# Gate and up of both feed-forward blocks by a seven-product scheme, the fourth product of a group ahead of the next group's sixth

## The chip, the cores and the metric

The kernel runs on one core of a Trainium2 chip. The metric is the device time of one execution in microseconds (us), the median of several runs; lower is better. The core has TensorE (matrix products, with weight loads of its own), VectorE (DVE in the rows), ScalarE (ACT), GpSimd (POOL) and SyncE (SP), whose queue starts most DMA transfers. Each engine works through its instructions in order; engines wait for each other on semaphores.

## What is computed

The reference is one step of a hybrid decoder layer on 512 prompt tokens and 8 sample tokens (520 columns here), width 1024. The change touches the two feed-forward blocks only:

```python
def swiglu_half(x, g_pre, w_gate, w_up, w_down, g_post):
    h = rmsnorm(x, g_pre)
    y = (jax.nn.silu(h @ w_gate) * (h @ w_up)) @ w_down
    return x + 0.5 * rmsnorm(y, g_post)
...
xp = swiglu_half(xp, *ffn1)
xp, sp = token_mixing(xp, ...)
xp = swiglu_half(xp, *ffn2)
```

The hidden width is 2816, that is 22 groups of 128 columns of w_gate and w_up. Everything is 32-bit.

## The kernel before

Activations lie transposed: x is [128 partitions, 8 chunks of 128 channels, 520 tokens]. TensorE multiplies in a 32-bit format of less precision, so every operand is held as a high part (a rounded copy, made by ScalarE) and a low part (the difference, made by VectorE), and every product is three: high x high, high weight x low, low weight x high. The norm factor of a token is applied after the products, to gate and to the hidden value.

`ffn(which, ...)` (from line 447) is one feed-forward block, called for which = 0 and 1 with the mixer between. Its weights come as blocks of [128, 8 x 128] (512 KB), gate and up in turn; the down projection has 16 blocks of [128, 11 x 128] (704 KB). A block goes through these steps, all by the block's number: `load_block` (L108) on SyncE's queue, into one of two raw buffers `w_raw`, as soon as the low part of the block two before is made; `split_high` (L129) on ScalarE; `split_low` (L133) on VectorE; `block_products` (L150, L152, L154) on TensorE: for each of 8 chunks, 2 token halves x 3 products of 260 columns into two PSUM banks, 48 matmuls a block, 96 for gate and up of one group.

Per group VectorE takes gate times factor out of PSUM (L592), ScalarE makes silu (L514), GpSimd multiplies by the factor again (L493), VectorE multiplies with up (L602), ScalarE makes the high part `a_high` (L518), VectorE the low part (L607). The first two groups are written out, the 20 others are a rolled loop (`pe.Fori(2, KF)` and its counterparts on the other engines). With the first block `start_products` (L288 to L292) takes the first group as its inputs come in. The `down` loop follows, then a second norm and the residual; x stays in SBUF throughout a block.

## Time and profile before

| | us |
|---|---|
| median of 3 runs | 1528.04 (1527.54 to 1530.77) |
| the profiled execution, first to last instruction (span) | 1525.5 |
| TensorE busy | 1485.0 (97%), 12552 matmuls |
| weight loads of TensorE busy (beside the matmuls) | 1367.5 (90%) |
| VectorE busy | 670.1 (44%) |
| ScalarE busy | 494.4 (32%) |
| GpSimd busy | 209.9 (14%) |
| rolled gate and up groups, first and second block | 230.7 each |

No time of the profiled execution besides its span is recorded; the median of the runs is 2.5 us above it. "Busy" counts the time in which an engine has at least one instruction under way; matmuls overlap each other, so their mean duration is more than what one of them adds. The share of an engine is a mean over stages with different limits. The granted clock of TensorE is 0.990 of 2.4 GHz on the mean.

### The profile page before, as it was taken

What the parts mean: (1) busy time and instruction counts of PE and PEld (TensorE: products, weight loads), DVE (VectorE), ACT (ScalarE), POOL (GpSimd) and SP (SyncE); (2) the same over time, 40 slices, a digit from 0 to 9 for tenths busy, and PEclk for the clock granted to TensorE, in tenths of its full rate; (3) what the DMA queues carried; (4) which work ended last, traced back from release to release, by engine and by line L of the source; (5) the groups of instructions that cost most, each with busy time, mean ns of one, the idle gap of its engine ahead of it and who ended that gap; (6) DMA issues with size and microseconds to landing.
All of it is one profiled execution on the core that took longest, in us unless ns stands there. A gap on an engine that the chain in (4) does not pass through costs nothing. (4 is left out here: it accounts for less than half of the span.)

```text
span 1525.5 us, 31235 instructions
## 1 busy us (share of the span) xinstructions
PE 1485.0 (97%) x12552; PEld 1367.5 (90%) x12552; DVE 670.1 (44%) x1021; ACT 494.4 (32%) x724; POOL 209.9 (14%) x199
## 2 busy tenths in 40 slices
PE   8999999999999999999998999989999999999996
PEld 7999999999888888877876887769989999999996
DVE  5333333222645765244476533456364434433224
ACT  6222223222521345221134333342353322323222
POOL 0111111000162000323200220021001111110000
PEclk9999999999999999999999999989999999999998
DMA  4222223222569978999997667837213222232221
GB/s 160 94 96 82 96 88 106 96 95 82 198 230 359 327 272 288 368 329 334 380 344 252 198 210 253 283 129 261 84 47 105 84 96 86 93 99 97 95 95 56
DMA packets 113366, 268.80 MB, mean 176 GB/s; under 512 B 15562, under 2 KB 18251, under 8 KB 112515
## 3 DMA queue, kind: packets, MB, share of 16 engines
q1 hardware_dynamic: 106610, 243.27, 46.5%
q0 software_dynamic: 6240, 23.28, 4.3%
q8 instruction: 64, 1.05, 0.3%
q10 hardware_dynamic: 432, 1.05, 0.2%
q14 instruction: 20, 0.16, 0.0%
HBM read 253.29 MB, written 14.26 MB: 175 GB/s over the span
## 5 line engine op out<-in xcount | busy, mean ns | idle before, releaser
L129 ACT ACTIVATE w_high<-w_raw 128x1024 fp32r<-128x1024 f32 (+1 forms) x179 | 199.6, 1116 | 705.6 <-PE psum L154 680.4
L133 DVE TENSOR_TENSOR w_low<-w_raw,w_high 128x1024 fp32r<-128x1024 f32 (+1 forms) x179 | 231.8, 1296 | 431.6 <-ACT w_high L129 430.2
L150 PE MATMUL psum<-h_high,w_high 128*128 128x260 f32 x1344 | 270.6, 282 | 0.6 <-DVE w_low L133 0.6
L154 PE MATMUL psum<-h_high,w_low 128*128 128x260 f32 x1344 | 270.9, 283 | 0.0
L152 PE MATMUL psum<-h_low,w_high 128*128 128x260 f32 x1344 | 270.4, 283 | 0.0
L150 PEld LDWEIGHTS psum<-h_high,w_high 128*128 128x128 f32 x1344 | 207.2, 188 | 1.5 <-DVE w_low L133 1.5
L154 PEld LDWEIGHTS psum<-h_high,w_low 128*128 128x128 f32 x1344 | 207.2, 188 | 0.0
L152 PEld LDWEIGHTS psum<-h_low,w_high 128*128 128x128 f32 x1344 | 206.6, 188 | 0.0
L493 POOL TENSOR_TENSOR silu<-silu,factor 128x520 f32<-128x520 f32 x44 | 79.1, 1798 | 505.3 <-ACT silu L514 505.3
L150 PE MATMUL psum<-mix_h_high,w_high 128*128 128x260 f32 x672 | 140.5, 290 | 1.2 <-issue 1.2
L152 PE MATMUL psum<-mix_h_low,w_high 128*128 128x260 f32 x672 | 136.4, 284 | 0.9 <-issue 0.9
L154 PE MATMUL psum<-mix_h_high,w_low 128*128 128x260 f32 x672 | 136.5, 285 | 0.4 <-issue 0.4
L150 PE MATMUL psum<-a_high,w_high 128*128 128x260 f32 x660 | 133.1, 283 | 0.0
L154 PE MATMUL psum<-a_high,w_low 128*128 128x260 f32 x660 | 132.7, 282 | 0.0
L152 PE MATMUL psum<-a_low,w_high 128*128 128x260 f32 x660 | 132.5, 282 | 0.0
L150 PEld LDWEIGHTS psum<-mix_h_high,w_high 128*128 128x128 f32 x672 | 104.3, 190 | 18.0 <-issue 17.6
L154 PEld LDWEIGHTS psum<-mix_h_high,w_low 128*128 128x128 f32 x672 | 104.8, 190 | 1.2 <-issue 1.2
L152 PEld LDWEIGHTS psum<-mix_h_low,w_high 128*128 128x128 f32 x672 | 104.7, 190 | 0.4 <-issue 0.4
L152 PEld LDWEIGHTS psum<-a_low,w_high 128*128 128x128 f32 x660 | 101.8, 188 | 0.0
L154 PEld LDWEIGHTS psum<-a_high,w_low 128*128 128x128 f32 x660 | 101.6, 188 | 0.0
L150 PEld LDWEIGHTS psum<-a_high,w_high 128*128 128x128 f32 x660 | 101.5, 188 | 0.0
L1058 POOL DMA_INDIRECT scores<-in_cache_logf,logf_rows x64 | 66.8, 1043 | 24.1 <-issue 17.7
(366 smaller groups left out, 2003.4 us busy)
## 6 DMA issues: line engine op xcount, KB each, us to landing
kv_ring<-in_cache_k SPq DMA_DIRECT2D x256, 256.0 KB
kv_ring<-in_cache_v SPq DMA_DIRECT2D x256, 256.0 KB
w_raw<-in_w_gu SPq DMA_DIRECT2D x86, 512.0 KB
w_raw<-in_w_dn SPq DMA_DIRECT2D x32, 704.0 KB
w_raw<-in_w_proj SPq DMA_DIRECT2D x44, 512.0 KB
spill<-h_f POOLq DMA_DIRECT2D x20, 260.0 KB
gates<-spill POOLq DMA_DIRECT2D x16, 260.0 KB, 4.2
w_raw<-in_w_merge SPq DMA_DIRECT2D x8, 512.0 KB
```

The costliest lines, as they stand in the source:

```text
L129: act.activation(w_high[:, u, 0:nk, :], w_raw[:, u, 0:nk, :], ACT.Copy).then_inc(high_done, 1)
L133: dve.tensor_tensor(w_low[:, u, 0:nk, :], w_raw[:, u, 0:nk, :], w_high[:, u, 0:nk, :].bitcast(F32), ALU.subtract).then_inc(low_done, 1)
L150: pe.matmul(out[h], w_high[:, u, k, :], high[:, k0 + j, tok[h]], start=s, stop=False)
L152: pe.matmul(out[h], w_high[:, u, k, :], low[:, k0 + j, tok[h]], start=False, stop=False)
L154: mm = pe.matmul(out[h], w_low[:, u, k, :], high[:, k0 + j, tok[h]], start=False, stop=e)
L493: pool.tensor_tensor(sg[:, u, :], sg[:, u, :], factor[:, :], ALU.mult).then_inc(gate_late, 1)
L1058: pool.indirect_dma_start(sc[:, t * P + 1:(t + 1) * P + 1], None, a["cache_logf"], bass.IndirectOffsetOnAxis(ap=idx[:, r, t:t + 1], axis=0 ...
```

## The change

Of each group n from 2 to 21, the product of the weights (gate and up, each cut into even and odd chunks) with the activations (even and odd chunks, each cut into two token halves) is a product of 2 x 2 blocks. The eight block products become seven, in the manner of Strassen and Winograd, with sums of weights and of activations made beforehand and sums of results behind:

- P1 and P2 (together "PA", 24 matmuls), P3, P4, P5, P6, P7 (12 matmuls each): 84 a group. P1 and P2 use the even and odd chunks of gate with the first half of the tokens.
- Sums of weights: S1, S2 (VectorE), S3, S4 (GpSimd), each 4 x 128 columns. Each unit's high part is made by ScalarE (`unit_high`) and its low part by VectorE (`unit_low`), in a ring of 4 slots of 4 chunks, PA in 8 chunks of its own.
- Sums of activations t(0) to t(3), once per block, by GpSimd out of `xw` (x times the norm weights, made by ScalarE), each 4 x 260 columns, then high and low parts.
- Sums of results: g1 = P1 + P2, u2 = P1 + P6, c22, c12 on VectorE and ScalarE; silu and factor in halves of 260 columns ("g1f", "silu1", "late1", "g2f", "silu2", "c22f"); the hidden value in halves ("hid1", "hid2").
- Order on TensorE for each n: PA(n), P7(n-1), P5(n), P4(n-1), P6(n), P3(n-1).
- All steps are counted on one semaphore per engine (`gu_act`, `gu_dve`, `gu_pool`, `gu_used`); A, V, G and at give the count behind a step. The rolled loops become straight-line code. The raw weights, their parts and the half results lie over `w_raw`, `w_high`, `w_low`, x, `h_f`, `root` and `sq`; x is therefore loaded again behind the stage, and in the second block written to DRAM before it.
- The start of the down projection is rewritten to fit (`down_start`), and the mixer's merge counts on other semaphores, with the same steps.

The core of the diff:

```diff
+def unit_order():
+    order = [("gate", 1), ("up", 1)]
+    for n in range(G0, KF + 1):
+        for kind, m in (("PA", n), ("P7", n - 1), ("P5", n), ("P4", n - 1), ("P6", n), ("P3", n - 1)):
+            if G0 <= m < KF:
+                order.append((kind, m))
+    return order
...
+def ring_slots(order):
+    slot, free, r, held = {}, {}, 0, []
+    for i, (kind, n) in enumerate(order):
+        if kind in ("gate", "up"):
+            at = (0, 0)
+        elif kind == "PA":
+            at = (0, 8)
+        else:
+            c = 8 + 4 * ((r - 5 * NG7) % 4)
...
+BANK_A = {n: (n + 2) % 3 for n in range(G0, KF)}
+BANK_B = {n: 5 + n % 2 for n in range(G0, KF)}
+BANK_C = {n: 3 + n % 2 for n in range(G0, KF)}
...
-            nb = n0 + 2 * KF
+            nb = n0 + 2
...
+                c_raw = over(f"second_raw{which}", [P, 2, KD, P], F32, ah, 2 * T)
+                c_high = over(f"second_high{which}", [P, 2, KD, P], F32R, ah, 6 * T)
+                c_low = over(f"second_low{which}", [P, 2, KD, P], F32R, al, 2 * T)
+                sg = over(f"silu{which}", [P, 2, T], F32, ah, 10 * T)
+                xw = over(f"x_weighted{which}", [P, KD, T], F32, ah, 12 * T)
+                hf = over(f"hidden{which}", [P, 2, T], F32, al, 6 * T)
+                t2 = over(f"sum_two{which}", [P, KD // 2, HT], F32, al, 8 * T)
...
+                raws = [over(f"raw_even{which}", [P, 2, KD, P], F32, "w_raw"),
+                        over(f"raw_odd{which}", [P, 2, KD, P], F32, "x", 4 * T)]
...
+                def operand(kind, j):
+                    if kind == "P1":
+                        return h_high[:, 2 * j, first_half], h_low[:, 2 * j, first_half]
+                    if kind == "P2":
+                        return h_high[:, 2 * j + 1, first_half], h_low[:, 2 * j + 1, first_half]
+                    if kind == "P3":
+                        return h_high[:, 2 * j + 1, second_half], h_low[:, 2 * j + 1, second_half]
+                    if kind == "P7":
+                        return h_high[:, 2 * j, second_half], h_low[:, 2 * j, second_half]
+                    if kind == "P5":
+                        return t_hi[:, j, :], t_lo[:, j, :]
+                    if kind == "P6":
+                        return t_hi[:, 4 + j, :], t_lo[:, 4 + j, :]
+                    return t_hi[:, 8 + j, :], t_lo[:, 8 + j, :] if j < 2 else t4_rest[:, j - 2, :]
...
-                    load_stream(sp, w_gu, 2 * KF, n0, KD, first=False)
-                    load_stream(sp, w_dn, 2 * KD, nb, NKD)
...
+                    sp.wait_ge(low_done, n0 + 2)
+                    load(G0, 0)
+                    load(G0, 1)
+                    if which == 1:
+                        for k in range(KD):
+                            sp.wait_ge(x_new, r0 - KD + k + 1)
+                            sp.dma_start(a["x_spill"][:, k, :], x[:, k, :]).then_inc(x_back, 16)
+                        sp.wait_ge(x_back, 32 + 16 * KD)
+                    sp.wait_ge(h_low_done, m0 + KD)
+                    sp.wait_ge(norm_sq, (norm_n + 1) * KD)
+                    sp.wait_ge(gu_act, A("xw", KD - 1))
+                    load(G0 + 1, 0)
+                    load(G0 + 1, 1)
+                    for n in range(G0 + 2, KF):
+                        sp.wait_ge(gu_pool, G("S4", n - 2))
+                        load(n, 0)
+                        sp.wait_ge(gu_dve, V("P4", n - 2))
+                        load(n, 1)
+                    sp.wait_ge(gu_pool, G("S4", LAST - 1))
+                    sp.wait_ge(gu_dve, V("P4", LAST - 1))
+                    load_block(sp, w_dn, 0, nb, 0, NKD)
+                    sp.wait_ge(gu_used, at("PA", LAST))
+                    load_block(sp, w_dn, 1, nb + 1, 1, NKD)
+                    sp.wait_ge(gu_dve, V("low", LAST))
+                    sp.dma_start(x[:, :, :], a["x"] if which == 0 else a["x_spill"]).then_inc(x_back, 16)
+                    load_stream(sp, w_dn, 2 * KD, nb, NKD, first=False)
...
+                    def sum_three(n):
+                        pool.wait_ge(gu_in[2 * (n % 2)], arrived(n))
+                        pool.wait_ge(gu_in[2 * (n % 2) + 1], arrived(n))
+                        if n > G0:
+                            pool.wait_ge(gu_dve, V("P7", n - 1))
+                        pool.tensor_tensor(s34[:, 0, :, :], even(gate(n)), even(up(n)), ALU.subtract).then_inc(gu_pool, 1)
...
+                    def sum_four(n):
+                        pool.wait_ge(gu_dve, V("S2", n))
+                        if n > G0:
+                            pool.wait_ge(gu_dve, V("P3", n - 1))
+                        pool.tensor_tensor(s34[:, 1, :, :], s12[:, 1, :, :], odd(gate(n)), ALU.subtract).then_inc(gu_pool, 1)
...
+                    pool.wait_ge(gu_act, A("xw", KD - 1))
+                    pool.tensor_tensor(xe1, xe1, xe2, ALU.subtract).then_inc(gu_pool, 1)
+                    pool.wait_ge(gu_pool, G("t", 0))
+                    pool.tensor_tensor(t2[:, :, :], xo2, xe1, ALU.add).then_inc(gu_pool, 1)
+                    late(0)
+                    pool.wait_ge(norm_rec, norm_n + 1)
+                    sum_three(G0)
+                    pool.tensor_tensor(xe2, xo2, xe2, ALU.subtract).then_inc(gu_pool, 1)
+                    late(1)
+                    pool.wait_ge(gu_pool, G("t", 1))
+                    pool.tensor_tensor(xo1, xo1, t2[:, :, :], ALU.subtract).then_inc(gu_pool, 1)
+                    sum_four(G0)
+                    for n in range(G0, KF):
+                        if n >= G0 + 2:
+                            gate_second(n - 2)
+                        if n > G0:
+                            sum_three(n)
+                            sum_four(n)
+                        gate_first(n)
+                        if n > G0:
+                            up_second(n - 1)
+                        gate_first_late(n)
...
+                    def unit_high(kind, n):
+                        slot, free = SLOT[kind, n], FREE[kind, n]
+                        if free:
+                            act.wait_ge(gu_used, u0 + free)
...
+                    def second_sum(n):
+                        act.wait_ge(gu_used, at("P6", n))
+                        if n >= G0 + 2:
+                            act.wait_ge(gu_dve, V("c12", n - 2))
+                        act.activation(u2[n % 2], psum[:, BANK_A[n], 0:HT], ACT.Copy).then_inc(gu_act, 1)
...
+                    silu(0)
+                    high(0)
+                    act.wait_ge(block_used, n0 + 2)
+                    unit_high("PA", G0)
+                    sum_high(0, t_hi[:, 0:4, :], xe1)
+                    unit_high("P5", G0)
+                    sum_high(1, t_hi[:, 4:8, :], t2[:, :, :])
+                    silu(1)
+                    unit_high("P6", G0)
+                    high(1)
+                    act.wait_ge(gu_used, at("up", 1))
+                    sum_high(2, T3_HIGH, xe2)
+                    sum_high(3, t_hi[:, 8:12, :], xo1)
+                    if which == 1:
+                        act.wait_ge(x_back, 32 + 16 * KD)
+                    for n in range(G0, KF):
+                        second_product(n)
+                        if n >= G0 + 2:
+                            gate_second_silu(n - 2)
+                        if n > G0:
+                            unit_high("P3", n - 1)
+                        if n < LAST:
+                            unit_high("PA", n + 1)
+                        unit_high("P7", n)
+                        gate_first_silu(n)
+                        fifth_product(n)
+                        second_sum(n)
+                        if n < LAST:
+                            unit_high("P5", n + 1)
+                        if n >= G0 + 2:
+                            hidden_high(n - 2)
+                        if n < LAST:
+                            unit_high("P6", n + 1)
+                        unit_high("P4", n)
...
+                    def sum_one(n):
+                        dve.wait_ge(gu_in[2 * (n % 2) + 1], arrived(n))
+                        if n > G0:
+                            dve.wait_ge(gu_dve, V("P5", n - 1))
+                            dve.wait_ge(gu_dve, V("S2", n - 1))
+                        dve.tensor_tensor(s12[:, 0, :, :], even(up(n)), odd(up(n)), ALU.add).then_inc(gu_dve, 1)
...
+                    def up_second(n):
+                        dve.wait_ge(gu_used, at("P7", n))
+                        dve.wait_ge(gu_act, A("p5", n))
+                        dve.tensor_tensor(c22[n % 2], psum[:, BANK_A[n], 0:HT], c22[n % 2], ALU.subtract).then_inc(gu_dve, 1)
...
+                    for n in range(G0, KF):
+                        gate_first(n)
+                        if n >= G0 + 2:
+                            hidden_second(n - 2)
+                        if n < LAST:
+                            sum_one(n + 1)
+                        if n > G0:
+                            up_second(n - 1)
+                            unit_low("P3", n - 1)
+                        if n < LAST:
+                            unit_low("PA", n + 1)
+                        unit_low("P7", n)
+                        if n < LAST:
+                            unit_low("P5", n + 1)
+                        if n >= G0 + 2:
+                            hidden_low(n - 2)
+                        if n < LAST:
+                            sum_two(n + 1)
+                        if n > G0:
+                            hidden_first(n - 1)
+                        if n < LAST:
+                            unit_low("P6", n + 1)
+                        if n > G0:
+                            gate_second(n - 1)
+                        unit_low("P4", n)
...
+                    def products(kind, bank, slot, j, start):
+                        hi, lo = operand(kind, j)
+                        out = psum[:, bank, 0:HT]
+                        pe.matmul(out, wh[:, slot, :], hi, start=start, stop=False, skip_group_check=True)
+                        pe.matmul(out, wh[:, slot, :], lo, start=False, stop=False, skip_group_check=True)
+                        return pe.matmul(out, wl[:, slot, :], hi, start=False, stop=j == 3, skip_group_check=True)
...
+                    def unit(kind, n):
+                        slot = SLOT[kind, n]
+                        pe.wait_ge(gu_dve, V(kind, n))
...
+                            for j in range(4):
+                                products("P1", BANK_A[n], slot + 2 * j, j, j == 0)
+                                mm = products("P2", BANK_B[n], slot + 2 * j + 1, j, j == 0)
...
+                            elif kind == "P6":
+                                pe.wait_ge(gu_dve, V("g1", n))
...
+                            elif kind == "P7":
+                                pe.wait_ge(gu_act, A("u2", n))
...
+                                if kind == "P4":
+                                    pe.wait_ge(gu_dve, V("c22", n))
```

## Rows read from the trace of the kernel before

**Rows 1.** Windows: busy us of each engine in the first rewritten stretch, then PEclk, DMA share, GB/s
```profile
33.90:264.60 230.70, 230.70 (x1923) 230.70 (x1922) 89.49 (x100) 66.01 (x80) 36.69 (x20) 1.00 0.28 94
```

**Rows 2.** Timeline (start us, us, what, [idle <-releaser]): TensorE in the loop; VectorE and TensorE at 1141
```profile
102.95 0.40 PE L154 MATMUL psum<-h_high,w_low 128*128 128x260 f32 x2
103.19 0.40 PE L150 MATMUL psum<-h_high,w_high 128*128 128x260 f32 x2
...
1141.02 1.23 DVE L133 TENSOR_TENSOR w_low<-w_raw,w_high 128x1024 fp32r<-128x1024 f32 x1 [0.49 <-ACT w_high L129]
1142.30 0.51 PE L150 MATMUL psum<-h_high,w_high 128*128 128x260 f32 x2 [0.58 <-DVE w_low L133]
```

**Rows 3.** Groups by form (xcount | busy us, mean ns | idle): VectorE, then ScalarE
```profile
L133 DVE TENSOR_TENSOR w_low<-w_raw,w_high 128x1024 fp32r<-128x1024 f32 x147 | 179.8, 1224 | 255.6 <-ACT w_high L129 254.2 <-issue 1.4
L133 DVE TENSOR_TENSOR w_low<-w_raw,w_high 128x1408 fp32r<-128x1408 f32 x32 | 52.0, 1625 | 176.0 <-ACT w_high L129 176.0
L435 DVE SCALAR_TENSOR_TENSOR x<-h_f,x 128x260 f32<-128x260 f32 x16 | 6.9, 428 | 0.6
L232 DVE TENSOR_TENSOR w_low<-w_raw,w_high 128x512 fp32r<-128x512 f32 x1 | 0.7, 683 | 0.0
...
L129 ACT ACTIVATE w_high<-w_raw 128x1024 fp32r<-128x1024 f32 x147 | 155.5, 1059 | 530.7 <-PE psum L154 505.5 <-remote 14.5 <-DMA w_raw<-in_w_merge 6.6
L1337 ACT ACTIVATE fox_probs_t<-psum 128x256 f32<-128x256 f32 x8 | 3.0, 380 | 5.9 <-PE psum L2123 5.9
```

**Rows 4.** Timeline of ScalarE, VectorE, GpSimd and SyncE in the loop of gate and up
```profile
103.45 1.06 ACT L129 ACTIVATE w_high<-w_raw 128x1024 fp32r<-128x1024 f32 x1 [4.24 <-PE psum L154]
...
109.16 1.06 ACT L129 ACTIVATE w_high<-w_raw 128x1024 fp32r<-128x1024 f32 x1 [2.02 <-PE psum L154]
110.25 1.23 DVE L133 TENSOR_TENSOR w_low<-w_raw,w_high 128x1024 fp32r<-128x1024 f32 x1 [0.31 <-ACT w_high L129]
110.82 1.82 POOL L493 TENSOR_TENSOR silu<-silu,factor 128x520 f32<-128x520 f32 x1 [9.73 <-ACT silu L514]
111.65 0.33 SPq L108 DMA_DIRECT2D w_raw<-in_w_gu  x1
```

**Rows 5.** A window while one block lands, and DMA issues (xcount, KB each, us to landing)
```profile
114.00:114.50 0.50, 0.50 (x7) 0.50 (x6) 0.00 (x0) 0.00 (x0) 0.00 (x0) 1.00 0.62 246
...
x<-x_spill SPq DMA_DIRECT2D x1, 2080.0 KB, 8.9
o_y<-x SPq DMA_DIRECT2D x16, 130.0 KB, 1.7
w_small<-in_w_small SPq DMA_DIRECT2D x1, 384.0 KB, 3.1
```

**Rows 6.** GpSimd: timeline with VectorE idle, and one line's durations (ns min/median/max)
```profile
27.04 1.30 POOL L493 TENSOR_TENSOR silu<-silu,factor 128x520 f32<-128x520 f32 x1 [26.22 <-ACT silu L514]
...
L1138 POOL TENSOR_TENSOR silu_z<-silu_z,proj x8: 717/725/768, 1002.0 to 1006.9; 128x256 f32<-128x256 f32 x6, 128x272 f32<-128x272 f32 x2
```

**Rows 7.** Timeline and windows of TensorE around two falls of the granted clock
```profile
432.23 0.41 PE L150 MATMUL psum<-mix_h_high,w_high 128*128 128x260 f32 x2 [0.90 <-issue]
436.17 0.64 PE L152 MATMUL psum<-mix_h_low,w_high 128*128 128x260 f32 x2
434.00:434.50 0.50, 0.12 (x1) 0.14 (x1) 0.00 (x0) 0.00 (x0) 0.00 (x0) 0.67 0.19 57
441.00:441.50 0.50, 0.50 (x6) 0.50 (x6) 0.00 (x0) 0.00 (x0) 0.50 (x1) 1.00 1.15 492
...
815.35 0.66 PE L2174 MATMUL psum<-ident,proj 128*128 128x128 f32 x4 [1.95 <-DVE attn_t L1792]
816.00:817.00 1.00, 1.00 (x10) 1.00 (x8) 0.62 (x1) 0.95 (x2) 0.00 (x0) 0.73 0.00 0
```

**Rows 8.** Timeline of ScalarE at the two norm factors
```profile
24.37 0.64 ACT L185 ACTIVATE factor<-root 128x520 f32<-128x520 f32 x1
...
1139.92 2.00 ACT L129 ACTIVATE w_high<-w_raw 128x1024 fp32r<-128x1024 f32 x2
```

More of the change, by code:

```diff
@@ L50 @@
 SLOTS = 25
+G0 = 2
+NG7 = KF - G0
+def unit_order():
[14 more added lines that the diff above has]
+            c = 8 + 4 * ((r - 5 * NG7) % 4)
+            at = (c, c + 4)
+            r += 1
+        slot[kind, n] = at[0]
+        free[kind, n] = max([k + 1 for k, b in enumerate(held) if b[0] < at[1] and at[0] < b[1]], default=0)
+        held.append(at)
+    return slot, free
@@ new lines, in pool_steps @@
+def pool_steps():
+    last = KF - 1
+    s = [("t", 0), ("t", 1), ("late", 0), ("S3", G0), ("t", 2), ("late", 1), ("t", 3), ("S4", G0)]
+    for n in range(G0, KF):
+        s += [t for t in (("g2f", n - 2), ("S3", n), ("S4", n), ("g1f", n), ("c22f", n - 1), ("late1", n))
+              if G0 <= t[1] < KF and (n > G0 or t[0] not in ("S3", "S4"))]
+    return s + [("g2f", last - 1), ("c22f", last), ("g2f", last)]
+ACT_STEPS, DVE_STEPS, POOL_STEPS = [act_steps(0), act_steps(1)], dve_steps(), pool_steps()
```

469 lines of the change are left out of this document (361 added, 108 removed).

## Prediction

> **What bounds the kernel now.** I read the stages by windows first. The two stretches that the change rewrites, the 20 rolled groups of gate and up in each feed-forward block (33.9 to 264.6, and 1153.8 to 1384.5 with the same busy time), have TensorE busy without a gap at full clock, 230.7 us each, or 11.535 us a group of 96 matmuls [rows 1]. The timeline of TensorE tells what a matmul costs: pairs of 260 columns start 0.24 us apart, so 0.120 us each; the pair's 0.40 overlaps the next and is no price [rows 2]. Then the helpers: a VectorE step of 512 columns lasts 0.68 us (520 as much within 0.02), of 1024 1.22, of 260 0.43. ScalarE takes 1.06 for 1024, 0.38 for 256 out of PSUM, and by the line between the two 0.61 for 512 [rows 3]. A step's last 0.08 lies beside the next one. Last the handoffs: ScalarE starts 0.26 us after TensorE's next block does (103.19 to 103.45) [rows 2, 4]; VectorE 0.03 after ScalarE ends (110.22 to 110.25) [rows 4]; TensorE 0.05 after VectorE (1142.25 to 1142.30), and its first pair takes 0.1 more [rows 2].
>
> **What is saved.** Seven products for eight: 84 matmuls a group instead of 96, so 10.08 us, if nothing waits. 40 groups x 12 x 0.120 = 57.6 us. Everything else is what the helpers make of it. Per group VectorE gets 14 steps: 7 of 512, one of 1024, 5 of 260, one of 520, 8.9 us busy; ScalarE 12 steps, 6.9 us; GpSimd 6 steps. None is over 10.08 by its sum. So the order counts, and I follow one loop of it.
>
> **The loop that sets the period.** Zero is the start of ScalarE's "u2"(n), released by the end of P6(n). ScalarE is in order: P5(n+1) high from 0.29 to 0.90. VectorE is in order too, so all its later steps stand behind this wait: P5 low 0.93 to 1.62, low(n-2) 1.54 to 2.24, S2(n+1) to 2.85. ScalarE P6(n+1) high 2.90 to 3.51; VectorE P6 low 3.54 to 4.23, c12(n-1) to 4.58, P4(n) low to 5.19. Only now may the queue of SyncE load up(n+2): the raw buffers are two deep and P4(n) is the last reader. And the third step of VectorE's next iteration, S1(n+2), needs that block. It stands ahead of c22(n), which P4(n) on TensorE waits for, so the whole latency of a load lies on the path.
>
> The price of that load of 512 KB: VectorE ends at 111.48, SyncE issues at 111.65 [rows 4], and bytes still flow at 246 GB/s in the mean of 114.0 to 114.5 [rows 5]. A store of 130 KB takes 1.7 us from issue to landing, a load of 384 KB 3.1 [rows 5]. I take 0.17 + 3.1 us (2.9 to 3.5). Landed at 8.46; S1 8.5 to 9.19, c22 9.11 to 9.54; TensorE starts P4(n) at 9.70. Meanwhile it has done P3(n-1), PA(n+1), P7(n), P5(n+1), 60 matmuls, until 6.94, and stands for 2.8 us. P4(n) and P6(n+1), 24 matmuls, 2.88 us, end at 12.58; the next u2 starts at 12.84. So the period is **12.8 us** by TensorE's branch, not 10.08, and over the 11.535 of today.
>
> **Two things lengthen it.** First GpSimd. From c22(n) a second branch leads to u2(n+1): P3 low ends 10.15, GpSimd S4(n+1), g1f(n+1), ScalarE silu1, p5, u2. A GpSimd step of 520 columns takes 1.30 us where VectorE stands still [rows 6] and 1.82 where its first 0.66 us lie beside a VectorE step on two SBUF operands (110.82 to 111.48) [rows 4]; 256 columns take 0.72 [rows 6]. So beside VectorE it loses 0.8 of the shared time. S4 (512 columns, 1.29 alone) meets PA low and P7 low for 1.7 us: 1.29 + 1.35, until 12.84; g1f 0.73, silu1 0.42, p5 0.3: u2 at **14.3 us**. With no such loss it would be 13.0, with a full stop 14.7. The row decides for 14.3.
> The Trainium skill ("SBUF — State Buffer", Who interferes with whom) says the same port pair is an exclusive lock between GpSimd and a VectorE step with two SBUF inputs, for whichever comes first. By that rule S4 waits to the end of P7 low, and the period would be 14.7 us and the kernel 14 us slower than I say; it would hold VectorE's steps back as well, which no row here shows.
>
> Second the clock. After pauses of TensorE that add up to some 2 us between 431.3 and 434.2 (0.90 ahead of 432.23 is one), the granted clock went from 1.00 to 0.50, that is from 2.4 to 1.2 GHz, at 434.2 and was back at 441.0; after one pause of 1.95 us it fell too, between 816 and 817 [rows 7]. A pause of 2.8 us or more in each period is over both after which it fell. At 1.2 GHz a pair lasts 0.64 us for 0.40 and starts 0.43 behind the one before, for 0.24 [rows 2, 7]: the 24 matmuls of TensorE's branch then cost up to 2.3 us more, and about 1.2 if the fall comes late in them. That branch gives 14.1 to 15.2. Both lengthenings lie on parallel branches, so they don't add; I take **14.5 us** a period.
>
> **The sum**, per feed-forward block, from the end of the second group's products to the first product of down (230.7 us today):
> - Start. In the first block ScalarE makes x_weighted after the factor (25.0) [rows 8]: 8 x 0.65, until 30.2. GpSimd then does two sums of 1040 columns, 2.6 us each at the rate of 1.30 for 520, ahead of late(0), 1.3: 36.7. Hidden, high, PA high, PA low (0.7, 0.64, 1.06, 1.22) put PA(2) at 40.4, where TensorE is free at 33.9. Two more sums, late(1) behind silu(1), t high and g1(2) put P6(2) at 51 to 55. u2(2) starts 22 us behind the free point (19.6 to 25). In the second block x_weighted is interleaved with the residual and done by 1139.9, when ScalarE turns to the next weights [rows 8]: 12.5 us (10.8 to 15).
> - First period 12.8 (VectorE has fewer steps), 17 full ones 246.5, one without a load 11.3, and P3, P7, P4, P3 with a wait for c22(21) that nothing covers any more, 6.4: 277.0.
> - So 299.0 and 289.5, that is +68.3 and +58.8.
> - Down: x must come back (2080 KB) ahead of the third weight block, behind "low"(21). It landed in 8.9 us beside other loads [rows 5]; at the 492 GB/s peak of a window [rows 7] the bytes alone are 4.3. The block is loaded behind it and split (1.4 by ScalarE's line, 1.62) [rows 3], and is ready 18 to 21 us after the first product of down; TensorE wants it after two blocks of 66 matmuls, 15.8: 2.2 to 5.3, 4.5 with the clock, twice: +9.
> - The rest at nothing: the merge's renamed semaphores count the same events, the spill of x before the second block moves to hidden queue time. Its cover is 11.5 us of products; if that failed it would cost what is left of 8.9. Unrolled loops: straight-line code paused for "issue" by 0.9 us a few times [rows 7]; 0 to 5 us, taken as 0.
> +136 on a span of 1525.5 gives 1661.6; the median of the runs lies 2.5 above the span: **1664 us**.
>
> **The rivals.**
> 1. Clock stays up and GpSimd keeps its pace: period 12.84, starts 19.6 and 10.8, down 2.2 each. 17 x 12.84 + 11.4 + 10.1 + 6.2 = 246.0, so 265.6 and 256.8: +35 + 26 + 4 = +65, **about 1595**; anything between it and mine is a part of the groups falling. For it: the clock needs TensorE to have stood at the right moment, and GpSimd's rows are of other shapes. Against it: [rows 4, 6, 7]. Chance 0.19.
> 2. TensorE stays the bound (the other side, faster): the loop closes inside 10.08 us. It decides at a period of about 11.1; below it the groups gain more than starts and down lose. The load would have to land 1.5 us after its issue, when VectorE comes to S1 behind hid2 (c12, g2f, silu2, hid2: 4.58 to 6.9), and the handoffs that I read would have to be much shorter. All waits hidden gives -57.6 + 13.6 + 5 (starts) + 1.5 (ends) + 5 (down): **1495**. Against it: 3.1 us landing, and VectorE 88% full by its own sum. Chance 0.08.
> 3. Only the load is hidden: S1 6.9, c22 7.9, P4 8.0, next u2 at 11.2. 17 x 11.2 + 10.5 + 10.1 + 6.2 = 217.2, with the short starts 236.8 and 228.0 for 230.7, down 4: +7.4, **1535**, or no change if a start is shorter. Chance 0.05.
> Mine: 0.68.
>
> **How the numbers follow.** Range: low 1592, rival 1 nearly whole; high 1705, from 15.4 us a period (17 x 0.9 x 2 = 31), the long starts (5) and down (5). This leaves out rivals 2 and 3 and a little on both sides. Faster by over 0.2% (3 us, about what a measurement of this kernel can tell from no change) 0.08, within 0.02, slower 0.90 (the rest of rival 3, rival 1 and mine).
>
> **What would show it.** Right: in the rewritten stretch TensorE idles once a group, before the line of P4, 2.5 to 3.5 us, released by VectorE; S1 on VectorE shows a wait for the load of w_gu; the granted clock is 0.5 in a good part of the stretch; GpSimd's S4 lasts 2.0 us or more. Wrong: S1 without a wait (rival 2); a clock of 1.00 with a period under 13.2 (rival 1); no wait of VectorE ahead of P5 low. The forecast is off if loads land much sooner than 3.1 us alone, or if GpSimd holds VectorE back, which would lift it above the range.

## The result and the profile after

The changed kernel takes 1687.7 us (median of 4 runs, 1684.0 to 1692.0), the kernel before on the same chip 1527.8 (1527.5 to 1530.8): ratio 1.105, interval 1.103 to 1.107. It is 160 us slower; the forecast was 136 slower, 1664, and the time lies inside the forecast range of 1592 to 1705. The profiled execution took 1684.0 with a span of 1682.2; its mean granted TensorE clock is 0.956 (0.990 before).

The page of the changed kernel: busy time by engine, TensorE's busy tenths and clock in 40 slices, and one group of its products by line (xcount | busy us, mean ns | idle before them and what ended it). L1149 is the first of the three matmuls of a chunk in the new stretch.

```profile
PE 1489.5 (89%) x12072; PEld 1361.4 (81%) x12072; DVE 900.5 (54%) x1393; ACT 620.7 (37%) x1070; POOL 437.5 (26%) x407
...
PE   6687877789999999999998999989978877877997
...
PEclk9889999999999999999999999989989899999998
...
L1149 PE MATMUL psum<-sums_high,gu_high 128*128 128x260 f32 x480 | 157.6, 328 | 122.6 <-DVE halves L1000 110.6
```

Where [rows 1] showed 230.7 us of TensorE without a gap, the slices now show 7 and 8 tenths, and the clock of several slices is under full. Of 122.6 us of idle time ahead of the products on sums, 110.6 were ended by L1000 on VectorE, "c22". The waits of TensorE, then of VectorE (us in total, times, longest us):

```profile
PE psum L1149 <- DVE halves L1000: 110.6, 40, 4.2
PE psum L1149 <- DVE silu L944: 13.2, 2, 11.3
PE psum L233 <- DVE w_low L216: 8.8, 2, 4.9
...
PE psum L1211 <- DVE w_low L1080: 4.3, 2, 2.2
```

```profile
DVE sums_up L973 <- DMA raw_even<-in_w_gu: 28.6, 18, 3.3
DVE sums_up L973 <- DMA raw_odd<-in_w_gu: 23.9, 18, 1.5
```

40 groups, 40 waits for c22: that is the wait ahead of P4. VectorE in turn waited at S1 (L973) for the raw weights, 52.5 us in 36 groups. One period in the timeline (start us, us, engine, line, out<-in, [idle before <-releaser]), from one S1 and c22 to the next:

```profile
153.82 0.69 DVE L973 TENSOR_TENSOR sums_up<-raw_even 128x512 f32<-128x512 f32 x1 [1.35 <-DMA raw_even<-in_w_gu]
154.43 0.42 DVE L1000 TENSOR_TENSOR halves<-psum,halves 128x260 f32<-128x260 f32 x1
155.00 0.36 PE L1149 MATMUL psum<-sums_high,gu_high 128*128 128x260 f32 x1 [3.46 <-DVE halves L1000]
...
155.59 2.14 POOL L708 TENSOR_TENSOR sums_gate<-sums_up,raw_odd 128x512 f32<-128x512 f32 x1 [3.42 <-DVE gu_low L990]
156.50 1.78 DVE L990 TENSOR_TENSOR gu_low<-sums_gate,gu_high 128x512 fp32r<-128x512 f32 x1
157.69 1.19 POOL L712 TENSOR_TENSOR halves<-halves,factor 128x260 f32<-128x260 f32 x1
158.92 0.42 ACT L814 ACTIVATE halves<-halves 128x260 f32<-128x260 f32 x1 [5.56 <-POOL halves L712]
159.51 0.38 ACT L836 ACTIVATE second_sum<-psum 128x260 f32<-128x260 f32 x1
...
168.31 0.69 DVE L973 TENSOR_TENSOR sums_up<-raw_odd 128x512 f32<-128x512 f32 x1 [1.44 <-DMA raw_odd<-in_w_gu]
168.92 0.42 DVE L1000 TENSOR_TENSOR halves<-psum,halves 128x260 f32<-128x260 f32 x1
```

c22 at 154.43, P4 released at 155.00 after 3.46 us of standing. GpSimd's S4 (L708) takes 2.14 us where 512 columns alone take 1.29, its factor on g1 (L712) 1.19 for 0.74; P7 low on VectorE (156.50) takes 1.78 us for 0.69. ScalarE's silu1 (L814) waits 5.56 us for GpSimd, and u2 (L836) stands behind it. At the end S1 waits 1.44 for the load. The next c22 is at 168.92: a period of 14.49. In the first block 17 periods in a row take 247.1 us, 14.54 each (the first 13.86, one 15.56, the others 14.3 to 14.7).

Two neighbouring periods in the chain of work that ended last (start us, us, what). The first goes over GpSimd, the second over TensorE:

```profile
1416.83 3.44 DMA raw_odd<-in_w_gu
1421.33 0.61 DVE gu_low L990
1422.07 2.14 POOL sums_gate L708
1424.21 1.16 POOL halves L712
1425.98 0.38 ACT halves L836
...
1431.23 3.47 DMA raw_even<-in_w_gu
1435.90 0.36 PE psum L1149
...
1439.96 0.21 PE psum L1151
...
1440.86 0.63 ACT gu_high L810
```

In the second chain the last products start 0.21 apart, not 0.12: the clock has fallen there. So either of two branches can end last between c22 and u2, and they are nearly as long as each other.

### The profile page after: what moved, and what is told of

It is laid out like the page before. It is cut to its first block and busy times, and to the rows that moved or that the text cites. A ratio compares the mean times of both kernels' runs of the same rounds, so it can differ in the third digit from the quotient of the medians.

```text
span 1682.2 us, 31039 instructions
## 1 busy us (share of the span) xinstructions
PE 1489.5 (89%) x12072; PEld 1361.4 (81%) x12072; DVE 900.5 (54%) x1393; ACT 620.7 (37%) x1070; POOL 437.5 (26%) x407
## 5 line engine op out<-in xcount | busy, mean ns | idle before, releaser
L1149 PE MATMUL psum<-sums_high,gu_high 128*128 128x260 f32 x480 | 157.6, 328 | 122.6 <-DVE halves L1000 110.6
L1149 PEld LDWEIGHTS psum<-sums_high,gu_high 128*128 128x128 f32 x480 | 108.0, 225 | 132.4 <-DVE halves L1000 117.9
L1149 PE MATMUL psum<-h_high,gu_high 128*128 128x260 f32 x640 | 184.2, 288 | 14.1 <-DVE silu L944 13.2
L1150 PE MATMUL psum<-h_low,gu_high 128*128 128x260 f32 x640 | 183.4, 287 | 0.0
L1151 PE MATMUL psum<-h_high,gu_low 128*128 128x260 f32 x640 | 182.8, 286 | 0.0
L1151 PE MATMUL psum<-sums_high,gu_low 128*128 128x260 f32 x480 | 152.2, 317 | 0.0
L1149 PEld LDWEIGHTS psum<-h_high,gu_high 128*128 128x128 f32 x640 | 123.5, 193 | 15.1 <-DVE silu L944 13.6
L1150 PE MATMUL psum<-sums_low,gu_high 128*128 128x260 f32 x400 | 124.6, 312 | 0.0
L1150 PEld LDWEIGHTS psum<-h_low,gu_high 128*128 128x128 f32 x640 | 123.2, 192 | 0.0
L1151 PEld LDWEIGHTS psum<-h_high,gu_low 128*128 128x128 f32 x640 | 123.1, 192 | 0.0
L1151 PEld LDWEIGHTS psum<-sums_high,gu_low 128*128 128x128 f32 x480 | 108.4, 226 | 0.0
```

The source lines that it names most:

```text
L1149: pe.matmul(out, wh[:, slot, :], hi, start=start, stop=False, skip_group_check=True)
L1150: pe.matmul(out, wh[:, slot, :], lo, start=False, stop=False, skip_group_check=True)
L1151: return pe.matmul(out, wl[:, slot, :], hi, start=False, stop=j == 3, skip_group_check=True)
```

## Experiments

All of them are read with one ruler: the starts of c22(n-1) (VectorE), of the u2(n) behind it (ScalarE), and of the next c22, from the timelines of the first block. "Period" is the median from one u2 to the next over 17 groups. Times of single profiled executions, unless "median" is said; the kernel before took 1525.6 beside e1 to e4, 1522.1 beside e5 to e8, 1520.4 beside e9 and e10, 1521.0 beside e11 and e12 (the last two medians of 7 runs). Totals a few us apart tell nothing: the changed kernel's own four runs span 8 us, and the part that none of e1 to e7 edits, from the first product of the first down to the end of the second block's first two groups, took 898 to 901 us in the changed kernel and e1 to e4, and 892 in e5 to e7. So the period is the measure, and in close cases the length of the two rewritten stretches (305.4 + 295.2 us in the changed kernel). Lines of code are cut at their ends where they are long, and "..." stands for lines left out.

| kernel | us | c22 to u2 | period |
|---|---|---|---|
| changed | 1684.0 | 5.08 to 5.26, once 6.14 | 14.48 |
| e1 P6 ahead of P4 | 1683.2 | 5.07 to 5.11 | 14.44 |
| e2 S1 late | 1609.1 | 5.09 | 12.54 |
| e3 silu1 late | 1697.7 | 3.70, 4.9 to 5.25, 6.14 | 15.12 |
| e4 filled | 1679.1 | 5.09 | 14.16 |
| e5 e3 and e4 | 1659.8 | 3.65 | 13.74 |
| e6 e2, g1's factor ahead of S4 | 1592.9 | 3.70 | 12.33 |
| e7 e6, hid2 late | 1612.8 | 3.88, 5.4 after a fall | 12.90 |
| e8 e7, start, reload | 1601.1 | as e7 | 12.90 |
| e9 e6, GpSimd cut | 1545.6 | 3.71 | 11.02 |
| e10 e6, VectorE's order, start, reload | 1562.2 median | 3.70 | 11.68 |
| e11 e10, hid1 earlier | 1549.3 median | 3.72 | 11.30 |
| e12 e11, GpSimd cut | 1500.0 | 3.80 | 10.08 |

### Which part of the loop sets the period: e1 to e5

**e1** undoes what the title names. One line of the order:

```diff
-        for kind, m in (("PA", n), ("P7", n - 1), ("P5", n), ("P4", n - 1), ("P6", n), ("P3", n - 1)):
+        for kind, m in (("PA", n), ("P7", n - 1), ("P5", n), ("P6", n), ("P4", n - 1), ("P3", n - 1)):
```

> The part of the change that its title names is undone: on TensorE the sixth product of group n+1 comes ahead of the fourth product of group n, so P6(n+1) no longer stands behind the wait for c22(n). All else is as in the changed kernel. In its trace the steady period, from one c22 to the next on VectorE, is 14.5 us. My theory: the period is set by the branch over GpSimd (P3 low, S4, the factor on g1, silu1, and only behind it u2 on ScalarE) and by the load ahead of S1, not by TensorE's order; u2 starts 159.51 there though the last product of P6 starts at 157.8. So period 14.5 +-0.15 and a total within 6 us of 1688. Rival (TensorE's order, as the first form of my sum had it with a fall of the clock): u2 comes as soon as P6 is done, some 1.5 to 2.9 us earlier a period, period 11.6 to 13, total 1580 to 1630.

Measured: 1683.2, period 14.44. The order in the title costs nothing here, and the run separates the two branches cleanly. P6 no longer waits for c22, so TensorE's branch is gone from between c22 and u2, while its clock still falls, in 9 of 18 windows. Two windows from c22 to u2 in e1 (window: length, PE busy (x matmuls) PEclk, DMA share, GB/s):

```profile
152.53:157.61 5.08, 4.51 (x37) 1.00 0.15 40
182.07:187.14 5.07, 4.50 (x25) 0.66 0.14 40
```

Clock 1.00 or 0.66, the length is 5.08: what is left is GpSimd's branch. In the changed kernel the same windows read:

```profile
212.45:217.53 5.08, 4.51 (x38) 1.00 0.14 37
226.85:232.10 5.25, 4.68 (x26) 0.67 0.17 39
95.42:101.56 6.14, 5.57 (x26) 0.50 0.25 87
```

Of the 18 steady ones in the first block of the changed kernel, 7 have the clock up and last 5.08 to 5.10, ten have 0.67 or 0.68 and last 5.12 to 5.26, and one has 0.50 and lasts 6.14.

**e2** takes S1, and with it the load, off the path. In VectorE's order (the issued steps follow it):

```diff
-(("g1", n), ("hid2", n - 2), ("S1", n + 1), ("c22", n - 1), ("P3", n - 1), ("PA", n + 1), ("P7", n),
+(("g1", n), ("hid2", n - 2), ("c22", n - 1), ("P3", n - 1), ("PA", n + 1), ("P7", n), ("S1", n + 1),
```

> S1(n+1) moves on VectorE from ahead of c22(n-1) to behind the low half of P7(n). With it go 1.4 us of waiting for the up weights' load and S1's own 0.69 us from the path c12, P4 low, load, S1, c22, P3 low, S4, g1's factor, silu1, u2, P5 high. My theory (load and GpSimd's branch in one loop): period 14.5 - 2.1 = 12.4, total 1688 - 2x18x2.1 = 1612 (1600 to 1630). Rival A (the load is hidden anyway, GpSimd's branch or the clock sets the period alone): 14.5, 1688 +-6. Rival B (the load still comes too late, now ahead of P5 high): 13.5 or more, 1650 or more.

Measured: 1609.1 and a period of 12.54, 1.94 less, for 2.1 expected. Rival A falls, and with it any account in which GpSimd or the clock alone makes the 14.5. VectorE's timeline in e2, one period:

```profile
150.37 0.41 DVE L1000 TENSOR_TENSOR halves<-psum,halves 128x260 f32<-128x260 f32 x1
...
154.15 1.23 DVE L973 TENSOR_TENSOR sums_up<-raw_odd 128x512 f32<-128x512 f32 x1
...
162.94 0.42 DVE L1000 TENSOR_TENSOR halves<-psum,halves 128x260 f32<-128x260 f32 x1
```

S1 has no wait any more; it takes 1.23 beside GpSimd. TensorE stands 1.4 and 0.6 us a period instead of 3.5, and the clock stays at 1.00 in every window from c22 to u2.

**e3** takes GpSimd's branch away from u2. In ScalarE's order:

```diff
-("P7", n), ("silu1", n), ("p5", n), ("u2", n), ("P5", n + 1),
+("P7", n), ("p5", n), ("u2", n), ("P5", n + 1), ("silu1", n),
```

> On ScalarE silu1(n) moves from ahead of p5(n) and u2(n) to behind u2(n) and the high half of P5(n+1). u2 then waits only for TensorE's products. My theory: in the trace of the changed kernel P6's last product starts 157.8 and ends near 158.1, u2 starts 159.51 behind silu1; the 1.4 us go, period 13.1, total 1688 - 2x18x1.4 = 1638 (1625 to 1655). Rival (TensorE's branch with its clock falls, as the prediction's step had it at 14.1 to 15.2, is as long): period 14.1 or more, total 1670 or more.

Measured: 1697.7, 14 us slower than the changed kernel, where I had written 46 faster. Windows from c22 to u2:

```profile
140.85:144.55 3.70, 3.14 (x26) 1.00 0.03 7
169.71:174.96 5.25, 4.68 (x26) 0.67 0.17 48
95.84:101.98 6.14, 5.58 (x26) 0.50 0.25 86
```

With the clock up the branch of TensorE is 3.70 us, as my sum had it (9.11 to 12.84). With a fall it is 5.25, with the clock down throughout 6.14, and one of the two was the case in 14 of 18: u2 waited for products now. silu1's later place also moved GpSimd's later steps onto VectorE's, and u2 to c12 went from 4.21 to 4.77. The rival named in the expectation was right.

**e4** keeps TensorE busy in the pause with matmuls that nothing reads, ahead of P4's wait for c22:

```diff
 if kind == "P4":
+    for _ in range(12):
+        pe.matmul(psum[:, 7, 0:P], ones[:, :], ones[:, :], start=True, stop=True)
     pe.wait_ge(gu_dve, V("c22", n))
```

> Twelve matmuls of 128 columns (24 passes, some 2.9 us at full clock) into a PSUM bank that is not in use are added on TensorE ahead of each P4's wait for c22(n); nothing reads them. They fill most of the 3.5 us in which TensorE waits there. My theory: TensorE's clock no longer falls, and the period stays at 14.5 since GpSimd's branch ends last; total within 6 us of 1688. Rival (falls of the clock set the period, my prediction's step of 14.1 to 15.2): with the clock up the period falls towards 12.8 to 13.5, total 1620 to 1655.

Measured: 1679.1, 5 us off, which is inside the spread of the changed kernel's runs; the two stretches are 2.3 us shorter. From c22 to u2 it is now GpSimd's 5.08 to 5.10 nearly always. The period fell by 0.32, more than the 0.1 to 0.15 that the clock can give there; the rest is between g1 and S1, 3.60 in the changed kernel and 3.32 here, so the loads landed earlier. Why they did I can't say. Three of 17 periods had loads later by 1.1 to 1.6.

**e5** does both:

> Both single edits at once: the twelve unused matmuls ahead of P4's wait (as in e4) and silu1(n) behind u2(n) and P5(n+1) high (as in e3). Theory after e3 and e4 (two branches of equal length lie between c22(n-1) and u2(n): GpSimd's, 5.1 us, and TensorE's, 3.7 us with its clock up, 5.2 us after one fall and 6.1 after two; taking away one leaves the other): c22 to u2 falls to 3.7 us, u2 to c12 stays at the 4.8 us of e3, so the period is 4.8 + 0.9 + 4.2 + 3.7 = 13.6, and the total 1688 - 2x17x0.9 = 1657 (1650 to 1665). Rival (silu1's later place itself costs what e3 lost, by late1 and hid1, whatever the clock): period near 14.6 or more, total 1690 or more. Rival (the clock alone counted): no better than e4, 1679.

Measured: 1659.8 for 1657. The total is 24 us under the changed kernel, but 7 of these are the unedited middle part. In the two rewritten stretches e3 alone lost 14.5 us, e4 alone gave 2.3, and both together gave 16.8. That is what two branches of nearly equal length look like: c22 to u2 is 3.65 throughout only when both are out of the way. What remains of the 13.7 is the rest of the loop, u2 to c12, P4 low and the load.

### What is behind it: e6 to e9

**e6** is e2 with GpSimd's order changed:

```diff
-("S3", n), ("S4", n), ("g1f", n), ("c22f", n - 1), ("late1", n)
+("S3", n), ("g1f", n), ("S4", n), ("c22f", n - 1), ("late1", n)
```

> On top of e2 (S1 behind P7 low) GpSimd's order is changed: the factor on g1(n) comes ahead of S4(n), so S4's 2.15 us no longer stand between c22(n-1) and u2(n). In e2's trace c22 to u2 is 5.09 us by GpSimd and TensorE waits 1.4 us once and 0.6 us once a period with its clock up. Theory: c22 to u2 falls to TensorE's 3.7 us, period 12.54 - 1.4 = 11.15, total 1609 - 2x18x1.4 = 1559 (1550 to 1572). Rival (the 2.15 us of S4 come back where they now fall, beside P5 low, a_low and S2, since VectorE and GpSimd stop one another): 11.9 to 12.5, total 1586 to 1609.

Measured: 1592.9. c22 to u2 fell to 3.70 as expected, but the period only to 12.33: the rival was right. (Of the 16 us under e2, 8 are the two stretches and the rest the unedited parts.) GpSimd and VectorE in e6, in order of their starts:

```profile
149.56 2.14 POOL L708 TENSOR_TENSOR sums_gate<-sums_up,raw_even 128x512 f32<-128x512 f32 x1 [0.69 <-DVE gu_low L991]
150.48 1.78 DVE L991 TENSOR_TENSOR gu_low<-sums_gate,gu_high 128x512 fp32r<-128x512 f32 x1
151.66 1.20 POOL L720 TENSOR_TENSOR halves<-halves,factor 128x260 f32<-128x260 f32 x1
152.18 1.23 DVE L974 TENSOR_TENSOR sums_up<-raw_odd 128x512 f32<-128x512 f32 x1
154.17 0.69 DVE L991 TENSOR_TENSOR gu_low<-sums_up,gu_high 128x512 fp32r<-128x512 f32 x1 [0.76 <-ACT gu_high L811]
...
156.83 0.69 DVE L991 TENSOR_TENSOR gu_low<-sums_up,gu_high 128x512 fp32r<-128x512 f32 x1 [0.42 <-ACT gu_high L811]
...
159.56 1.06 DVE L1022 TENSOR_TENSOR hidden_half<-halves 128x260 f32<-128x260 f32 x1 [0.76 <-ACT halves L819]
```

These VectorE steps now follow one another without a gap but for waits of 0.76, 0.42 and 0.76: the loop is VectorE's own queue, with three round trips to ScalarE and GpSimd in it. And the timelines tell how the two engines share. S4 starts at 149.56 while VectorE's PA low runs (149.34 to 150.55), and ends 1.15 after it; P7 low starts in name at 150.48 and ends 0.56 after S4; GpSimd's next step ends 0.60 after P7 low, and S1 0.55 after that. Alone these steps take 1.29, 0.69, 0.74 and 0.69 us. So each waits for the other engine's whole step and then needs its own length less 0.14: the engines take turns, and nothing is shared by halves.

**e7** moves hid2 out of the way of c22:

```diff
-(("g1", n), ("hid2", n - 2), ("c22", n - 1), ("P3", n - 1), ("PA", n + 1),
+(("g1", n), ("c22", n - 1), ("P3", n - 1), ("hid2", n - 2), ("PA", n + 1),
```

> On top of e6, hid2(n-2) moves on VectorE from ahead of c22(n-1) to behind the low half of P3(n-1). Its wait (0.75 us for silu2) and its 1.05 us no longer stand between g1(n) and c22(n-1). Theory: the loop shrinks by up to 1.8 us to 9.4, below what TensorE needs for 84 matmuls at 0.12 us (10.1), so TensorE's order sets the period: 10.1 to 10.7, total 1559 - 2x18x0.7 = 1534 (1525 to 1550). Rival (VectorE's own load, 9 to 10 us of work in the period of which up to 1.8 stands against GpSimd, becomes the bound, or the load, 5.5 us from P4 low to S1): 11 or more, total 1555 or more.

Measured: 1612.8, slower than e6 by 20. The wait for silu2 was not removed; P3 high stands behind silu2 on ScalarE, so P3 low waits 0.94 in hid2's stead. And S4 now came ahead of PA low: it ran from 153.49 to 154.97, and PA low, begun at 153.74, ended 1.08 behind it and took 2.31 us (1.21 in e6). The clock fell again in some periods, and they are no longer than the others (12.9 from c22 to c22 in either case): VectorE's queue is the bound.

```profile
152.14 0.79 DVE L991 TENSOR_TENSOR gu_low<-sums_gate,gu_high 128x512 fp32r<-128x512 f32 x1 [0.94 <-ACT gu_high L811]
...
153.74 2.31 DVE L991 TENSOR_TENSOR gu_low<-raw_odd,gu_high 128x1024 fp32r<-128x1024 f32 x1
```

**e8** adds the edits outside the loop: x reloaded by eight DMAs between the blocks of down, and scale(1) and PA(2) ahead of hid(0):

```diff
-sp.dma_start(x[:, :, :], a["x"] if which == 0 else a["x_spill"]).then_inc(x_back, 16)
-load_stream(sp, w_dn, 2 * KD, nb, NKD, first=False)
...
+for k in range(2):
+    sp.dma_start(x[:, k, :], x_src[:, k, :]).then_inc(x_back, 16)
+with sp.Fori(2, KD) as i:
+    for u in range(2):
+        load_block(sp, w_dn, i * 2 + u, i * 2 + (nb + u), u, NKD)
+    sp.dma_start(x[:, ds(i), :], x_src[:, ds(i), :]).then_inc(x_back, 16)
...
-[("silu", 0), ("high", 0), ("PA", G0), ("t", 0)
+[("silu", 0), ("PA", G0), ("high", 0), ("t", 0)
```

> e7 and three edits outside the steady loop: scale(1) and both halves of PA(2) come ahead of hid(0) and high(0) on their engines (in the changed kernel TensorE waits 11.3 us ahead of PA(2), until 45.8), and x is reloaded in eight parts between the blocks of the down weights instead of in one piece ahead of the third block (TensorE waited 3.9 and 4.9 us there). Theory: the reload gives 8 us, the start 3 to 6 us in each block since P5(2), P6(2) and P7(2) still wait for the sums on GpSimd and VectorE; total 1534 - 8 - 9 = 1517 (1505 to 1530), that is within 1% of the kernel before. Rival (the start is set by the sums t(0) to t(3) alone, and the reload in parts delays each block): 1530 or more.

Measured: 1601.1, 11.7 less than e7. The reload gave all of it and more: from the first product of the first down to the end of the second block's first two groups 891.8 became 884.9, from the second down to the end 148.1 became 141.2. PA(2) started at 36.7 instead of 45.9, yet the first u2 came at 58.84 instead of 57.38, since g1(2) still stood behind the sums t(2) and t(3) on VectorE. So the 11.3 us that TensorE waits for scale(1) are no loss of their own. The rival was right for the start, and wrong in that the reload in parts would delay each block.

**e9** tests the contention directly, on e6. Three GpSimd steps of a period are cut to one column; the other 511 and 2 x 259 columns are left out, so it isn't a complete kernel:

```diff
+pool.tensor_tensor(s34[:, 1, 0, 0:1], s12[:, 1, 0, 0:1], odd(gate(n))[:, 0, 0:1], ALU.subtract).then_inc(gu_pool, 1)
...
-pool.tensor_tensor(g1[n % 2], g1[n % 2], fac1, ALU.mult).then_inc(gu_pool, 1)
+pool.tensor_tensor(g1[n % 2][:, 0:1], g1[n % 2][:, 0:1], fac1[:, 0:1], ALU.mult).then_inc(gu_pool, 1)
...
-pool.tensor_tensor(c22[n % 2], c22[n % 2], fac2, ALU.mult).then_inc(gu_pool, 1)
+pool.tensor_tensor(c22[n % 2][:, 0:1], c22[n % 2][:, 0:1], fac2[:, 0:1], ALU.mult).then_inc(gu_pool, 1)
```

> e6 with three of GpSimd's steps of each period cut to one column (S4 but for the first group, the factor on c22, the factor on g1 behind silu1: 2.15, 1.20 and 1.20 us in e6's trace); their results are left out, all else is done. e6 missed its 11.15: its period is 12.33, a closed chain on VectorE from c22 to c22, in which P7 low takes 1.78 us (0.69 alone) beside S4, S1 1.23 (0.69) beside the factor on c22, P3 low 0.89 (0.69). Theory (VectorE and GpSimd stop one another): these steps fall back to about 0.69, the period to 12.33 - 1.09 - 0.54 - 0.20 = 10.5, total 1593 - 2x18x1.8 = 1528 (1520 to 1545). Rival (the long steps come from something else, such as their operands in h_f or the loads that land beside them): the period stays over 12.

Measured: 1545.6, period 11.02. The same steps as in e6:

```profile
151.40 1.04 POOL L708 TENSOR_TENSOR sums_gate<-sums_up,raw_odd 128x1 f32<-128x1 f32 x1 [0.69 <-DVE gu_low L993]
152.31 0.68 DVE L993 TENSOR_TENSOR gu_low<-sums_gate,gu_high 128x512 fp32r<-128x512 f32 x1
152.92 0.68 DVE L976 TENSOR_TENSOR sums_up<-raw_even 128x512 f32<-128x512 f32 x1
```

P7 low 1.78 became 0.68 and S1 1.23 became 0.68: 1.65 us, and the period fell by 1.31. P3 low stayed at 0.88, beside the first factor on g1, which was not cut. The steps of one column are not short: 1.04 us here and 0.65 for the two factors, each ending 0.05 to 0.06 us behind the VectorE step beside it. They too wait for the other engine's whole step, but then hold up nothing. What is missing of the expected 1.8 is this 0.2, and 0.3 by which VectorE now waits longer for P5 high (1.08 for 0.76).

### How far the scheme can go: e10 to e12

**e10** fills VectorE's waits with other steps, keeps e8's reload and start, and takes p2(2) and g1(2) ahead of t(2). Its order on VectorE, against e6:

```diff
-("P7", n), ("S1", n + 1), ("P5", n + 1), ("low", n - 2), ("S2", n + 1), ("hid1", n - 1), ("P6", n + 1), ("c12", n - 1), ("P4", n)
+("S1", n + 1), ("P7", n), ("S2", n + 1), ("P5", n + 1), ("P6", n + 1), ("c12", n - 1), ("P4", n), ("low", n - 2), ("hid1", n - 1)
```

> e6 and four more edits. VectorE's order in a period becomes g1, hid2, c22, P3 low, PA low, S1, P7 low, S2, P5 low, P6 low, c12, P4 low, a_low, hid1, so that the 0.76, 0.42 and 0.76 us which VectorE waits in e6 for P5 high, P6 high and silu2 are filled. x is reloaded in eight parts between the down weights. scale(1) and PA(2) come ahead of the first group's hidden, p2(2) and g1(2) ahead of the sums t(2) and t(3). Theory (VectorE's own queue is the loop after e6): period 12.33 - 1.5 to 1.9 = 10.4 to 10.8 against the 10.1 of 84 matmuls; total 1593 - 2x18x1.5 - 8 (reload) - 6 (start) = 1525 (1512 to 1540), level with the kernel before. Rival (with the waits filled, VectorE and GpSimd stop one another longer, as in e7): period 11.5 or more, total 1550 or more. Rival for the start: the first u2 stays where it was and only the reload gives its 8 us.

Measured: median 1562.2, ratio to the kernel before 1.028 (1.026 to 1.030); period 11.68, the rival's. **e11** takes "low" and "hid1" ahead of "P4":

> e10 with a_low(n-2) and hid1(n-1) ahead of P4 low(n) on VectorE. In e10's trace (period 11.69) ScalarE's p2(n) waits 2.95 us until hid1 has freed its buffer, and g1(n) and silu2 stand behind p2, so that VectorE waits 0.51 us again. Theory: that wait goes, period 11.1 to 11.2, total 1562 - 2x18x0.55 = 1542 (1535 to 1550), still slower than the kernel before. Rival (the time is VectorE's and GpSimd's work one after the other, whatever the order): 11.5 to 11.7, total 1555 to 1562.

Measured: median 1549.3, ratio 1.018 (1.016 to 1.020), period 11.30, between the two. In e11 VectorE waits only 0.16 us for another engine in a steady period; the three steps beside GpSimd's S4 and its two factors are these, each 0.69 alone (a fourth, hid2 beside S3, takes 1.19 for 0.42):

```profile
156.48 1.78 DVE L983 TENSOR_TENSOR sums_up<-raw_even 128x512 f32<-128x512 f32 x1
158.18 1.23 DVE L1000 TENSOR_TENSOR gu_low<-sums_gate,gu_high 128x512 fp32r<-128x512 f32 x1
159.33 1.23 DVE L992 TENSOR_TENSOR sums_up<-sums_up,raw_even 128x512 f32<-128x512 f32 x1
```

**e12** is e11 with the cut of e9, so it leaves the same results out:

> e11 with the three GpSimd steps cut to one column as in e9 (their results left out). Theory: what keeps e11 from TensorE's pace is the time in which GpSimd stops VectorE (S1 1.78, P7 low 1.23, S2 1.24, a_low 1.24 us in e10, each 0.69 alone, 2.8 us in all); with most of it gone the period is that of TensorE's 84 matmuls with small waits, 10.1 to 10.4, total 1542 - 2x18x0.85 = 1511 (1503 to 1522), less than the kernel before. Rival (the waits between engines, not the stops, hold it): 10.8 or more, total 1528 or more.

Measured: 1500.0, 21 us under the kernel before (one run). A long window in the steady groups of e11 and one of e12 (length, then busy us of TensorE, weight loads, VectorE, ScalarE and GpSimd, clock, DMA share, GB/s):

```profile
75.00:270.00 195.00, 177.85 (x1448) 174.57 (x1447) 189.15 (x242) 102.63 (x207) 141.52 (x104) 1.00 0.29 95
```

```profile
73.00:250.00 177.00, 177.00 (x1477) 177.00 (x1476) 153.73 (x242) 104.62 (x211) 103.48 (x107) 1.00 0.34 107
```

In e11 VectorE is busy 97% of the time. In e12 TensorE has no gap and the period is 10.08, the 84 matmuls at 0.120 us of my first step. So the saving in TensorE's work is real; what eats it in the best order that I found is VectorE, stopped by GpSimd. No complete kernel of these beat the one before.

## Why the prediction held, point by point

- **The saving**, 84 matmuls in 10.08 us if nothing waits: shown by e12, to the last digit.
- **TensorE's branch**, c22 to u2 in 3.73 us with the clock up: 3.70 (e3, e6). With falls I had up to 2.3 more, 1.2 for a late one: 4.9 to 5.25, and 6.14 when down throughout. Right, and the clock does fall at this pause, in 11 of 18 periods of the first block; over the whole stretch it is 0.91 on the mean.
- **GpSimd's branch**, 5.19 by my sum, by the factor of [rows 4]: 5.09. The size held by luck, and the mechanism was half of it. I let GpSimd lose 0.8 of the shared time and VectorE nothing, and wrote that no row shows VectorE held back. Here both are stopped: S4 lost 0.85 us, not 1.35, and the factor on g1 0.45, for which I had none; the two errors cancel. The row was misread: in [rows 4] GpSimd's step ends at 112.64, that is 1.16 us behind VectorE's and 0.14 under its length alone, just as S4 ends 1.14 behind PA low. It had stood still for VectorE's whole step, and what looked like 0.8 was a full stop less 0.14. P7 low lost 1.1, for which I had none either. That wasn't on the path in the changed kernel, since VectorE waited 2.16 us for P5 high afterwards; it became the bound in e6. The Trainium skill ("SBUF — State Buffer", Who interferes with whom) has the rule that the port pair is an exclusive lock for whichever comes first, and the trace agrees in kind: P7 low and S4 end one after the other. The 14.7 us that I drew from it was my misreading: S4 got its turn between PA low and P7 low and did not have to wait for the end of P7 low. The "14 us slower" was a slip as well: it counts 14.7 against 14.3, and against the 14.5 of the sum it is 7.
- **14.5 a period because two branches are parallel**: 14.54 over 17 periods, and e3, e4 and e5 show the tie. The load took 3.4 and 3.5 us from issue to landing, in place of 3.1; u2 to c22 was 9.3 us for 9.11.
- **The starts**: 22.2 and 14.1 for 22 and 12.5. The first came out by luck in part: PA(2) started at 45.8 and not at 40.4, since its products waited for scale(1), which I hadn't in the sum; e8 takes this wait away and gains nothing.
- **The first period**, which I had at 12.8 by "fewer steps", was 15.4 and 14.4, 4 us more in all. I had left out of it the two lengthenings that I put on the others: its c22 to u2 is 5.20 and 5.19, where 12.8 counts 3.73. In the first block c22 also came 10.2 us behind u2 for 9.11; what of that S2 makes (1.80 us for 0.69) was not tested.
- **The tail**: 9.3 a block for 6.4, 5.9 us in all and with down the largest miss. I had left out that the first product of down waits for its weights' low part behind the last groups' steps on VectorE: 2.16 and 2.14 us at L1211.
- **Down** took 7.4 us more than before in each block, for 4.5. The wait ahead of the third block, 3.90 and 4.87, was as I had it. The rest is the clock behind the pauses, of which my 4.5 had too little. In the changed kernel, behind the third block's wait (window: length, PE, PEld, DVE, ACT, POOL busy, PEclk, DMA share, GB/s):

```profile
361.42:365.00 3.58, 3.58 (x17) 3.58 (x18) 1.54 (x1) 0.87 (x2) 0.00 (x0) 0.52 0.70 214
1554.74:1558.00 3.26, 3.26 (x15) 3.26 (x16) 1.57 (x1) 0.90 (x2) 0.00 (x0) 0.50 0.63 197
```

  At 0.120 us a matmul these windows would hold 30 and 27. In the first down the clock fell once more, behind the 2.16 us pause ahead of its first product (0.67 from 339.91 to 343.00). The reload in parts gave 6.9 and 7.0 back (e7 to e8): without the waits the clock does not fall there either.
- **The sum**. Against the span of the profiled execution I was short by 20.6 us: 0.6 ahead of the first stretch, 6.4 and 5.7 in the two stretches, 5.0 between the first down and the second block (of which 2.3 is the wait for the second products' low part at 1225.56, VectorE beside GpSimd's 3.26 us sum), and 2.9 behind the second down. The last 3 us to the median are the spread of the runs: the profiled one was the fastest, and the median lies 5.5 above its span for my 2.5.
- **Rivals**. Rival 1 (1595) needed the clock up and GpSimd at its pace: e5 takes both away from between c22 and u2 and is still at 13.7 a period, since u2 to c12 grew from 4.2 to 5.2 when silu1's successors came beside VectorE's steps, and the load is there. Rival 3 (load hidden, 1535) had the right idea but the wrong price: e2 hides the load and gets 1609, since GpSimd's branch remained. Rival 2 was TensorE as the bound: only e12 shows it, which leaves results out.

What stays open: why the loads landed 0.3 us earlier in e4, and what makes c22 late in the first period of the first block.

## What to carry to other kernels

A scheme that saves TensorE's work and adds helper work is worth what the busiest helper leaves of it: lay out one period of every queue by durations that include what the engines do to each other, before counting matmuls. When two parallel branches tie, single edits show nothing or even a loss (e3, e4), and only the pair tells (e5). And a wait for a load at the head of an in-order queue holds up everything behind it; moving one step by a few places (e2) gave 75 us of the 160 back.

## What the runs showed of the hardware

VectorE steps with two SBUF operands and GpSimd steps exclude one another and take turns, step by step: 0.69 became 1.78 beside a GpSimd step of 512 columns and 1.23 beside one of 260. VectorE steps with one operand in PSUM (c22, g1, c12: 0.42) kept their time. GpSimd steps of a single column lasted 0.65 and 1.04 us, until the VectorE step beside them was over, but held VectorE up by nothing that shows (P7 low 0.68 in e9). A fall of the clock doubled the matmuls' spacing from 0.12 to 0.21, and cost nothing at all where another branch was as long (e1: 5.08 us from c22 to u2 at 1.00 and at 0.66).
